# Layer 3's and the differential attention worked in pairs of heads, their 64-row score products side by side, their loops unrolled

## The reference

```python
def diff_mixer(q, k, v, lam, subln_gain, lam_init, pos):
    ...
    def block(i):
        ...
        s = jnp.einsum('bqhmd,bshmd->bhmqs', qslice(q, i, Q_BLOCK), k).astype(jnp.float32) * B_QK_DIM ** -0.5
        causal = pos[None, :] <= t[:, None]
        p = safe_softmax(s, causal)
        a = p[:, :, 0] - lam_full * p[:, :, 1]
        return jnp.einsum('bhqs,bshe->bqhe', a.astype(v.dtype), v)
```

```python
def nsa_mixer(q, kc_raw, vc_raw, ks, vs, kw, vw, gates, pe, w1, w2, pos):
    ...
        g = qslice(gates, i, C_Q_BLOCK)
        return g[..., 0:1] * o_cmp + g[..., 1:2] * o_slc + g[..., 2:3] * o_win
```

## Time and profile before

| what | value |
|---|---|
| median of 3 runs | 3564.34 us (3557.97 to 3566.67) |
| the profiled execution's own time | 3554.38 us |
| its span, first to last instruction | 3552.6 us |
| TensorE busy, granted clock | 3217.9 us (91%), 0.935 |
| VectorE, ScalarE, GpSimd busy | 1791.1 us (50%), 1112.6 us (31%), 1091.1 us (31%) |
| differential attention, from 2154 to 2222 us | 68 us |
| layer 3's two causal attentions, from 2882.4 to 3109.7 us | 227.3 us |

### The profile page before, as it was taken

The page is one execution under the profiler, slowest core; times in us unless marked ns, Lnnn a source line. Parts: engine busy times, 40 slices in busy tenths (PEclk is TensorE's granted clock), DMA queues, the critical chain, the costliest instruction groups (busy, mean ns, idle before and its releaser), DMA issues.

```text
span 3552.6 us, 51190 instructions
## 1 busy us (share of the span) xinstructions
PE 3217.9 (91%) x16856; PEld 2541.6 (72%) x16856; DVE 1791.1 (50%) x3261; ACT 1112.6 (31%) x1951; POOL 1091.1 (31%) x683
## 2 busy tenths in 40 slices
PE   6778699999989898999978898899999988899997
PEld 3656578888867666998955655778777755578876
DVE  4665777753346664433436556342242366743324
ACT  3154242111141554422232123442222234543222
POOL 1121122323214112444423201244444322244443
PEclk9889899999999998999998886899999969999999
DMA  6101224433111001222221100223223100022222
GB/s 239 61 0 59 95 95 142 160 118 113 53 42 60 1 1 60 95 89 95 84 74 49 62 1 1 86 95 99 91 85 104 54 1 1 0 89 92 93 93 83
DMA packets 74337, 258.70 MB, mean 73 GB/s; under 512 B 9456, under 2 KB 12016, under 8 KB 72688
## 3 DMA queue, kind: packets, MB, share of 16 engines
q1 hardware_dynamic: 60256, 205.61, 17.6%
q10 hardware_dynamic: 13968, 51.65, 4.3%
HBM read 253.03 MB, written 2.10 MB: 72 GB/s over the span
## 4 chain that ended last, share of the span: by engine, by line
PE 81%; DVE 7%; issue 6%; ACT 3%; DVEq 1%; POOL 1%; DMA 1%; SPq 1%; ACTq 0%; POOLq 0%; PEldq 0%
PE ps L805 55%; PE ps L783 6%; PE ps L2253 3%; PE ps L2267 3%; PE ps L1466 2%; PE ps L1471 1%; PE ps L418 1%; DVE ps L381 1%; PE ps L2414 1%; PE ps L2446 1%; ACT w_hi L625 1%; PE ps L2408 1%; PE ps L2263 1%; PE ps L1078 1%; PE ps L2407 1%
## 5 line engine op out<-in xcount | busy, mean ns | idle before, releaser
L743 POOL TENSOR_TENSOR w_lo<-w_raw,w_hi 128x1024 fp32r<-128x1024 f32 (+1 forms) x373 | 918.8, 2466 | 1799.4 <-ACT w_hi L625 1799.4
L625 ACT ACTIVATE w_hi<-w_raw 128x1024 fp32r<-128x1024 f32 (+1 forms) x373 | 385.6, 1038 | 1233.2 <-PE ps L805 1000.6
L805 PE MATMUL ps<-h_hi,w_hi 128*128 128x258 f32 (+2 forms) x1824 | 324.2, 331 | 48.5 <-ACT w_hi L625 44.3
L805 PEld LDWEIGHTS ps<-h_hi,w_hi 128*128 128x128 f32 x1824 | 272.8, 195 | 87.4 <-issue 46.2
L805 PE MATMUL ps<-h_hi,w_lo 128*128 128x258 f32 (+2 forms) x1824 | 308.4, 321 | 0.0
L805 PE MATMUL ps<-h_lo,w_hi 128*128 128x258 f32 (+2 forms) x1824 | 307.1, 320 | 0.0
L805 PEld LDWEIGHTS ps<-h_hi,w_lo 128*128 128x128 f32 x1824 | 265.4, 190 | 27.6
L805 PEld LDWEIGHTS ps<-h_lo,w_hi 128*128 128x128 f32 x1824 | 263.6, 189 | 26.8
L1508 DVE TENSOR_REDUCE nm<-ps 128x1 f32<-128x512 f32 (+5 forms) x304 | 178.1, 586 | 93.7 <-PE ps L2255 45.5
L2253 PE MATMUL ps<-keys,qs 128*128 128x256 f32 (+3 forms) x672 | 178.5, 377 | 48.0 <-POOL qs L1434 42.0
L1565 ACT ACTIVATE probs<-ps,nm 128x512 f32<-128x512 f32 (+5 forms) x304 | 184.0, 605 | 111.5 <-DVE nm L1508 45.8
(11 more groups left out here) (327 smaller groups left out, 5226.0 us busy)
## 6 DMA issues: line engine op xcount, KB each, us to landing
w_raw<-in_ffn_in SPq DMA_DIRECT2D x176, 512.0 KB, 3.3
mod_row<-in_w_mod_rows ACTq DMA_DIRECT2D x80, 512.0 KB, 4.4
w_raw<-in_ffn_out SPq DMA_DIRECT2D x64, 512.0 KB, 3.3
w_raw<-in_ev_in SPq DMA_DIRECT2D x26, 512.0 KB, 3.3
w_raw<-in_ffn_out SPq DMA_DIRECT2D x32, 384.0 KB, 3.0
w_raw<-in_od_in SPq DMA_DIRECT2D x21, 512.0 KB, 3.4
mod_ring<-in_w_mod SPq DMA_DIRECT2D x8, 1024.0 KB, 13.0
w_raw<-in_wo_in SPq DMA_DIRECT2D x12, 512.0 KB, 3.3
```

The costliest lines, as they stand in the source:

```text
L625: act.activation(k.w_hi[:, s, 0:self.KT * P], k.w_raw[:, s, 0:self.KT * P], ACT.Copy).then_inc(k.sems["w_hi_ready"], 1)
L743: ins = pool.tensor_tensor(k.w_lo[:, s, 0:self.KT * P], k.w_raw[:, s, 0:self.KT * P], k.w_hi[:, s, 0:self.KT * P].bitcast(F32), ALU.subtract)
L805: ins = pe.matmul(k.ps[:, 2 * s + g, 0:t1 - t0], w[:, s, c * P:(c + 1) * P], h[:, c, t0:t1], start=(n == 0), stop=(n == len(parts) - 1))
```

## The change

A new class `PairAttend` takes the place of the differential attention's `Attend` and of all four `Attend` stages of layer 3, which become one stage of 16 turns. The compressed attention and the attentions of the first block and the latent one keep their code.

- The unit of work is a **pair**: both heads of one query tile. The scores are three products over 64 rows for each head, those of the two heads alternating, head 0 on rows 0 to 63 and head 1 on rows 64 to 127, into neighbouring banks, then the two masks. Keys and queries are read where they lie; `PadKeys` and the casts into `qs` are gone from these stages.
- One maximum and one reciprocal serve both heads, and one gate product. The exponential stays one for each head.
- Layer 3: head 0's tiles are turned round into bank 4 and copied by VectorE, head 1's into bank 5 and copied by ScalarE. The differential attention: the sum of both maps goes alternately to banks 4 and 5, and ScalarE copies all of it.
- TensorE runs two pairs ahead, in two pairs of banks. The values' products of a batch are issued as one piece, every second pair.
- In layer 3 VectorE writes the product with the spread to one of two `parts`, and GpSimd adds it to `o_t`.
- All loops of these stages are written out, with constants in every wait.

```diff
+class PairAttend(Stage):
...
+    def tensor(self, pe):
+        k, S = self.kit, self.kit.sems
+
+        def qk(p):
+            self.scores(pe, self.slot(p), p // QT, p % QT).then_inc(S["scores_ready"], 1)
+
+        def turn_round(p):
+            nt = p % QT + 1
+            if self.one:
+                pe.wait_ge(*self.count("prepared", p + 1))
+                if p >= 2:
+                    pe.wait_ge(*self.count("pt_b", p - 1))
+            for a in ((1,) if self.one else (0, 1)):
+                if not self.one and p >= 1:
+                    pe.wait_ge(*self.count("pt_b" if a else "pt_a", p))
+                for t in range(nt):
+                    ins = pe.transpose(k.ps[:, self.bank(p, a), t * P:(t + 1) * P], self.probs(p)[:, a, t * P:(t + 1) * P], k.ident[:])
+                ins.then_inc(S["tr_b" if a else "tr_a"], 1)
...
+        qk(0)
+        qk(1)
+        for p in range(self.N):
+            pe.wait_ge(*self.count("probs_ready", p + 1))
+            if p + 2 < self.N:
+                qk(p + 2)
+            turn_round(p)
+            if p >= 2 and p % 2 == 0:
+                output(p // 2 - 1)
+        output(self.B - 1)
...
+        for p in range(self.N):
+            dve.wait_ge(*self.count("probs_ready", p + 1))
+            chain.link(dve.reciprocal(self.rinv(p), k.rowsum[:, p % 2, :]))
+            self.prepare(dve, chain, self.rinv(p), self.probs(p), p // QT, p % QT).then_inc(S["prepared"], 1)
+            if p + 2 < self.N:
+                neg_max(p + 2)
+            if not self.one:
+                dve.wait_ge(*self.count("tr_a", p + 1))
+                dve.tensor_copy(self.turned(p, 0), k.ps[:, 4, 0:(p % QT + 1) * P].rearrange("p (t c) -> p t c", c=P)).then_inc(S["pt_a"], 1)
+            if p >= 3 and p % 2 == 1:
+                take((p - 3) // 2)
...
+        exp(0)
+        for p in range(self.N):
+            if p + 1 < self.N:
+                exp(p + 1)
+            if not self.one and p >= 3 and p % 2 == 1:
+                spread((p - 3) // 2)
+            act.wait_ge(*self.count("tr_b", p + 1))
+            act.activation(self.turned(p, 0 if self.one else 1), k.ps[:, self.bank(p, 1), 0:(p % QT + 1) * P].rearrange("p (t c) -> p t c", c=P), ACT.Copy).then_inc(S["pt_b"], 1)
...
+    def paired_scores(pe, s, qi, q_hi, q_lo, k_hi, k_lo):
+
+        q, n = slice(qi * P, (qi + 1) * P), (qi + 1) * P
+        for i, (lhs, rhs) in enumerate(((q_hi, k_hi), (q_hi, k_lo), (q_lo, k_hi))):
+            for a in range(2):
+                rows = slice(64 * a, 64 * a + 64)
+                pe.matmul(s[:, a, :], lhs[rows, q], rhs[rows, 0:n], start=(i == 0), stop=False, skip_group_check=True)
+        for a in range(2):
+            ins = pe.matmul(s[:, a, n - P:n], k.ident_b, k.causal, start=False, stop=True, skip_group_check=True)
+        return ins
...
-    PadKeys(k, [padded(i) for i in range(3)])
...
-            Attend(k, 4, [four(0), four(1)], scores, causal_tiles, lambda n, qi: 0,
...
+    PairAttend(k, len(turns3), scores3, pv3, gated, lambda dve, o, b: dve.tensor_tensor(k.parts[:, b % 2, :], o[:, 0:256], k.spread[:], ALU.mult),
+               k.pt_pair, False, add_part)
```

142 lines of the change are left out of this document (109 added, 33 removed).

## The result

The changed kernel takes 3476.35 us (median of 4 runs, 3470.02 to 3482.57), the kernel before, in the same comparison, 3564.7 us (3557.97 to 3566.67, 4 runs). The ratio is 0.9758, with a 95% interval of 0.9745 to 0.9772: 2.4% faster.

A forecast was written before the change was run, and what follows sets the result against it. The prediction took TensorE to bound the kernel, with 81% of the path. Layer 3 was to lose 47 us (27 turns, 20 borders), the differential attention 13; 3564.3 - 60 gave 3504 us, range 3483 to 3540.

The forecast's parts named there:

- Layer 3's borders: Layer 3: one stage start and end instead of four, with paddings and early casts gone, saves 20 of 47 us.
- TensorE's terms: Layer 3's turn on TensorE: scores 4.1, transposes 2.2, values and spread 3.3, together 9.6 us.
- a pair costs 0.54 + 3 streams: Score products of two heads overlap, three streams plus 0.54 us for changes, first load, lag and masks; 4.1 us a turn.
- The scores themselves gain nothing: Layer 3: paired score products with masks, 4.1 us a turn, cost no less than the old form.
- I put 1.2 us on these: Layer 3: TensorE's waits, lost preloaded weights and ScalarE's exponentials add 1.2 us to a turn, making 10.8 us.
- I take 55: Differential attention: 55 us, between 45 at 2.4 GHz and 61 at 1.2 GHz; 13 us less than 68.
- VectorE bounds it: Differential attention at 2.4 GHz: VectorE's work of 9.2 us sets the turn, 9.7 us with hand-offs.
- The two halves don't run side by side: Rival: paired score products need six streams, 1.95 us more a turn; layer 3 206 us, kernel 3536 us; chance 0.12.
- The hand-offs bound: Rival: TensorE waits through one ScalarE lump each turn of layer 3; 11.9 us a turn, 3522 us; chance 0.15.
- Everything fits: Rival: 10.2 us a turn in layer 3, differential attention at 2.4 GHz throughout, 45 us; kernel 3485 us; chance 0.15.
- The clock falls: Rival: 64-row products bring layer 3 to 1.2 GHz, turn 17.4 us, stage 286; kernel slower at 3616 us; chance 0.07.
- the fast rival: The rival "Everything fits": 10.2 us a turn in layer 3, kernel 3485 us; chance 0.15.

The follow-up runs named there:

- Experiment 3: The changed kernel with layer 3's sixteen turns in four stages of four instead of one stage; 3494.02 us, layer 3 185.3 us.
- experiment 6: The changed kernel with each head's 128-row mask right behind its own three score products, so a mask separates the heads; 3547.35 us.
- Experiment 9: The changed kernel with each double maximum of layer 3 computed twice on VectorE; 3509.34 us, layer 3 202.7 us.
- experiment 10: The changed kernel with VectorE copying head 0's transposed tiles before the double maximum two pairs ahead, layer 3's query tiles 0 and 1; 3473.43 us.
- experiment 5: The changed kernel with a pair's six score products ordered as head 0's three, then head 1's three, in both stages; 3478.72 us.
- experiment 11: The changed kernel with layer 3's reciprocal-spreading products moved out of the values' piece, behind the transposes of its second pair; 3474.93 us.

## Why the prediction was wrong in size

The forecast was 60 us, the two stages gave 82.2 and the medians 88. Step by step:

**Layer 3's borders: right.** "227.3 to 180, 20 from the borders" had 7 us left beside the turns. By the same cuts 163.1 - 16 x 9.79 = 6.5 us are left, for 27 before. Experiment 3 prices three borders at 18.5 us.

**TensorE's terms: right in kind, 0.3 us too high in sum.** The step "a pair costs 0.54 + 3 streams: 0.90, 0.90, 1.08, 1.23, together 4.1 us" was mis-sized. The pairs with their masks take 0.6, 0.77, 0.95 and 1.12 us, 3.4 in all. That the halves run side by side (three streams) was right, as experiment 6 shows by its opposite, and so were the streams: the second and third products start 0.11, 0.12, 0.17 and 0.23 us apart for the four tiles, for 0.12, 0.12, 0.18 and 0.23. Too high was the fixed part of 0.54. For the 512-wide pair the starts (2897.71, 2898.04, 2898.28, 2898.61, and 2898.73 for the transposes) leave 1.02 - 3 x 0.23 = 0.33 us, and 0.43 with the step into the 64 rows. The lag of the second half, which had some 0.1 us of it, is 3 to 9 ns. Two of the twelve changes aren't there, since a values' piece goes over into scores directly. Transposes were put at 2.2 and take 2.5 us, with some of the changes in them. Values and spread were put at 3.3 and take 3.3. The sum is 9.3 for 9.6. "The scores themselves gain nothing" was wrong: with their masks they take 0.9 us a turn less than before, by the starts. That bears on where the gain was looked for, and not on the 10.8 us.

**"I put 1.2 us on these": the step that failed most.** The place was right to the instruction: the transposes behind query tile 1 wait for the copy behind tile 3's maximum, 0.51 us, put at 0.4. What was wrong is all that was added to it for weights lost at waits and for ScalarE's exponentials: no such wait is there. TensorE has one wait a turn and not some five. Together 0.3 and 0.7 us make the turn 9.8 instead of 10.8, times 16 is 16 us: 47 forecast, 64 measured by the same cuts. Experiment 9 shows how far the other engines are from binding: of 3.3 us more for VectorE, 1.8 vanish, and nearly all of the rest comes in at the one place where TensorE already waits.

**The differential attention: the clock's share and VectorE's part were mis-sized.** The step "I take 55" put the stage between 45 us at 2.4 GHz and 61 at 1.2 GHz. It takes 50.3 by starts of products, 49 by the cuts. Turns are 11.3, 10.4 and 10.5 us. At 2.4 GHz VectorE was to bound the turn, with 9.2 us of work and 9.7 in all. VectorE's whole part in the chain of one turn, from one maximum of tile 3 (2189.50) to the next (2199.96):

```profile
2189.50 1.23 DVE nm L1687
2190.72 0.33 DVE qkv L2615
2191.32 0.34 DVE probs L2605
2191.68 0.63 DVE probs L2606
```

With the small pieces between, these are 2.8 us of 10.46; TensorE holds the rest, at a clock of 0.84 over the turn. VectorE is busy 8.2 us of it. So "VectorE bounds it" didn't come about: the two take turns on the path. A whole turn at 2.4 GHz is in no profile. A turn at 1.2 GHz was put at 13.8 us, and the first took 11.3, since the first rise to 2.4 GHz came within it.

**The remaining 6 us** of the 88 are in no stage of the change. At its median before has a rest of 3564.7 - 1.8 - 68.9 - 230.4 = 3263.6 us, the changed kernel 3476.35 - 1.8 - 50.3 - 166.8 = 3257.5 (the 1.8 and 1.9 us are own time less span). Both lie in the 3250 to 3264 us that the profiled builds show. In the profiled pair itself the rest goes the other way, 3253.3 to 3263.6. I take it for the spread of these other stages; that the change has no effect on them wasn't shown.

**The rivals.** *The two halves don't run side by side* is refuted by the starts 3 to 10 ns apart and by experiment 6, where it was forced. There it costs 71 us, where the rival had 32 over the forecast: 44 for 26 in layer 3, since eight changes and a longer start at 1.2 GHz come with it, and 24 for 6 in the differential attention, which loses its clock too. *The hand-offs bound* needed a lump of a us or more each turn; the waits show 0.55. *Everything fits* was nearest, with 10.2 us a turn; even this was 0.4 us too long. *The clock falls* didn't come about in layer 3: the steady part has 1.00, as before the change. Even with every score product alone on half the rows it has 1.00 there behind the start, and only the differential attention 0.57. The half-row products alone don't bring it down, then. The rule of the Trainium skill (TensorE: Matmul & The Clock Gate, Part 4) that transposes don't count as busy for the full clock found no effect in layer 3: 2.5 of 9.8 us are transposes, at 1.00. What sets the clock stays open. It is not TensorE's busy share alone: before had 0.58 in the differential attention with 63.4 of 68 us busy, and 1.00 in layer 3 with 41.3 of 47.8. Nor is the differential attention's clock a fixed thing of its code: experiment 10, which edits nothing there, had 0.74 for 0.70 over the whole stage, with the same length within 0.4 us.

The chances were sound for the sign (0.91 for faster), and the range was cut too close on the fast side: its lower end was the fast rival's 10.2 us a turn, when the sum's own terms, without the 1.2 us for waits, already gave 9.6.

## What to carry to other kernels

Where TensorE is the bound and every other engine is idle for a quarter of the turn or more, as here, work out each wait at its place and add nothing for the rest: the one computed wait was there, the lumped margin was not. What more work on another engine costs depends on where it stands, and not on that engine's idle time. Read an edit's worth from the length of its stage in the trace, which here repeats to a few tenths of a us where the whole program moves by 14, and look at the granted clock of the stage before dividing by the turns. Keep full-row products out from between the half-row products of a pair; the one other order of the six that was tried cost nothing. One long stage instead of four is worth more here (18.5 us) than the double maxima, reciprocals and gates (1.1 us in layer 3).

## What was not expected of the hardware

- Products on the two row halves run together even when they stand three instructions apart (experiment 5): starts at 2896.083 and 2896.093 us. One mask of 128 rows between them ends that (experiment 6), at 0.65 to 1.0 us a pair (the 512-wide pair, whose three products take 0.9 us a head, goes from 1.12 to 2.11 us).
- The granted clock of the differential attention goes with the pairing: 0.71 side by side, 0.57 one after the other, with the same products. Layer 3's steady clock of 1.00 holds in both, yet falls back nine times in the build where TensorE waits more for VectorE (experiment 9), and 12 us go with that.
- A small product on VectorE is held up while GpSimd adds. The gate's product over 2 columns takes 0.16 us alone and 0.53 when GpSimd's addition runs; with that addition on VectorE the mean falls from 331 to 162 ns. In the timelines of VectorE and of GpSimd the product that starts at 2895.63 ends at 2896.16, with the addition (2895.42 to 2896.14):

```profile
2895.63 0.53 DVE L2650 TENSOR_TENSOR rinv<-rinv,gates 128x2 f32<-128x2 f32 x1
...
2897.34 0.16 DVE L2650 TENSOR_TENSOR rinv<-rinv,gates 128x2 f32<-128x2 f32 x1
```

```profile
2895.42 0.72 POOL L2668 TENSOR_TENSOR o_t<-o_t,parts 128x256 f32<-128x256 f32 x1 [3.54 <-DVEq L1696]
```

The Trainium skill (SBUF — State Buffer, Who interferes with whom) has the rule: a VectorE instruction with two inputs in SBUF and a GpSimd instruction that reads SBUF lock each other out, and the later one waits for the whole of the other. The rows agree, with 0.53 us.

- One more change of the tile can pay: two a turn cost 0.3 us, and what they moved forward filled a wait of 0.55 (experiment 11).
